# VectorE's order in the FFN loops: the low part of the next w13 weights is moved to right behind u's low part, ahead of the two adaLN accumulates and w2's low part

## What is computed

```
def swiglu(h, w13, w2):
    a, b = jnp.split(h @ w13, 2, axis=-1)
    return (jax.nn.silu(a) * b) @ w2

for layer in range(DEPTH):                       # DEPTH = 2
    mod = (cond @ ada_w[layer] + ada_b[layer]).reshape(B_, N_MOD, D)      # cond = silu(c), N_MOD = 9
    h = modulate(rmsnorm(x, norm_g[layer, 0]), sh1, sc1)
    x = x + 0.5 * g1 * swiglu(h, ff_w13[layer, 0], ff_w2[layer, 0])
    h = modulate(rmsnorm(x, norm_g[layer, 1]), sh2, sc2)
    x = x + g2 * (even_mixer(h) or multiscale_pool(h))
    h = modulate(rmsnorm(x, norm_g[layer, 2]), sh3, sc3)
    x = x + 0.5 * g3 * swiglu(h, ff_w13[layer, 1], ff_w2[layer, 1])
```

## Time and profile before

| | us |
|---|---|
| median of 3 runs | 1084.23 |
| lowest, highest | 1082.85, 1085.43 |
| span of the profiled execution | 1077.9 |
| TensorE matmul busy in it | 979.4 (91%) |
| VectorE busy | 733.9 (68%) |
| ScalarE busy | 441.3 (41%) |
| loads from HBM | 237.54 MB |

### The profile page before, as it was taken

How to read it: one execution, slowest core, us unless ns; L and a number is a source line. 1 busy time by engine, 2 the same in 40 slices (tenths; PEclk the granted TensorE clock), 3 DMA queues, 4 the chain that set the end, 5 groups by cost and what they waited for, 6 DMA issues and landing times.

```text
span 1077.9 us, 17128 instructions
## 1 busy us (share of the span) xinstructions
PE 979.4 (91%) x6656; PEld 893.6 (83%) x6656; DVE 733.9 (68%) x843; ACT 441.3 (41%) x578; POOL 123.6 (11%) x182
## 2 busy tenths in 40 slices
PE   1598999998979898999999989989999879999998
PEld 1487899997969458998998969879989769999997
DVE  4966778678887544875867867668677675555544
ACT  1424343335536343543444444234333544443432
POOL 1110111102541101110101011101110010000000
PEclk9999999998989699899999989999999989999999
DMA  9986888886734022787887747868787416456441
GB/s 339 343 309 229 277 297 297 290 217 223 242 104 131 1 98 98 269 287 284 282 302 262 270 158 257 308 232 307 277 291 275 149 42 235 164 188 202 148 156 39
DMA packets 155690, 239.19 MB, mean 222 GB/s; under 512 B 14464, under 2 KB 124928, under 8 KB 155520
## 3 DMA queue, kind: packets, MB, share of 16 engines
q1 hardware_dynamic: 135056, 166.81, 46.0%
q0 software_dynamic: 19440, 71.31, 18.2%
q10 hardware_dynamic: 1152, 0.49, 0.2%
HBM read 237.54 MB, written 1.05 MB: 221 GB/s over the span
## 4 chain that ended last, share of the span: by engine, by line
PE 42%; DMA 25%; DVE 18%; issue 6%; ACT 5%; SPq 3%; POOL 1%; ACTq 0%; DVEq 0%; POOLq 0%
PE ps L1106 25%; DMA raw<-in_ff_w 24%; DVE lo L703 6%; DVE acc L744 4%; PE ps L1148 3%; PE ps L1147 3%; PE ps L1151 3%; SPq L296 2%; PE ps L1258 2%; DVE lo L709 1%; DVE x L793 1%; ACT arena L487 1%; PE ps L1261 1%; DVE xn L789 1%; ACT hi L455 1%
## 5 line engine op out<-in xcount | busy, mean ns | idle before, releaser
L1106 PE MATMUL ps<-hT_hi,hi 128*128 128x256 f32 x1408 | 402.0, 286 | 11.1 <-DVE lo L703 6.6
L1106 PE MATMUL ps<-hT_lo,hi 128*128 128x256 f32 x1408 | 400.5, 284 | 0.0
L1106 PE MATMUL ps<-hT_hi,lo 128*128 128x256 f32 x1408 | 400.3, 284 | 0.0
L1106 PEld LDWEIGHTS ps<-hT_hi,hi 128*128 128x128 f32 x1408 | 272.2, 193 | 19.4 <-DVE lo L703 10.5
L1106 PEld LDWEIGHTS ps<-hT_lo,hi 128*128 128x128 f32 x1408 | 272.4, 193 | 2.7
L1106 PEld LDWEIGHTS ps<-hT_hi,lo 128*128 128x128 f32 x1408 | 272.2, 193 | 0.0
L703 DVE TENSOR_TENSOR lo<-raw,hi 128x2048 fp32r<-128x2048 f32 (+1 forms) x110 | 243.8, 2216 | 16.2 <-ACT hi L455 15.5
L455 ACT ACTIVATE hi<-raw 128x2048 fp32r<-128x2048 f32 (+1 forms) x106 | 200.2, 1889 | 31.2 <-DMA raw<-in_ff_w 17.5
L511 ACT ACTIVATE hi<-raw 128x1024 fp32r<-128x1024 f32 x88 | 93.4, 1061 | 276.6 <-DMA raw<-in_ff_w 142.7
L720 DVE TENSOR_TENSOR u_lo<-u_buf,u_hi 128x256 fp32r<-128x256 f32 x88 | 37.3, 424 | 212.6 <-ACT u_hi L504 212.5
L744 DVE SCALAR_TENSOR_TENSOR acc<-ada,cond,acc 128x1024 f32<-128x1024 f32 x115 | 147.0, 1279 | 0.7
(11 more groups left out here) (126 smaller groups left out, 891.2 us busy)
## 6 DMA issues: line engine op xcount, KB each, us to landing
raw<-in_ff_w SPq DMA_DIRECT2D x86, 1024.0 KB, 7.6
ada<-in_ada_w POOLq DMA_DIRECT2D x132, 512.0 KB, 6.7
raw<-in_ff_w SPq DMA_DIRECT2D x92, 512.0 KB, 8.5
raw<-in_w_in SPq DMA_DIRECT2D x12, 1024.0 KB, 8.0
arena<-in_ada_w SPq DMA_DIRECT2D x4, 1024.0 KB, 18.8
raw<-in_w_out SPq DMA_DIRECT2D x4, 1024.0 KB, 6.3
raw<-in_ada_w SPq DMA_DIRECT2D x2, 1024.0 KB, 15.0
arena<-in_b_rpb SPq DMA_DIRECT2D x16, 128.0 KB, 4.2
```

Of the source, the lines that this page charges most:

```text
L1106: ins = mm(out, a, b, start=first and m == 0, stop=last and m == len(pairs) - 1)
```

## The change

In the loop body of VectorE's FFN, four instructions of each step change places. Before: `u_mul`, accumulate, `u_low`, accumulate, `w2_low`, `split_lo`. Now: `u_mul`, `u_low`, `split_lo`, accumulate, accumulate, `w2_low`. In FFN 3, without accumulates, only `w2_low` and `split_lo` change places. Nothing is added or removed, and the programs of the other engines and queues stay as they are, as do all waits.

```
                         u_mul(Q - 1, 4 * i, first=isinstance(i, int) and i + d == 0)
+                        u_low(Q - 1, 4 * i)
+                        split_lo(n0 + d + 2, 4 * i)
                         if with_ada:
                             ada_tile(m0, 2 * d, i, gates)
-                        u_low(Q - 1, 4 * i)
-                        if with_ada:
                             ada_tile(m0, 2 * d + 1, i, gates)
                         w2_low(Q, 4 * i)
-                        split_lo(n0 + d + 2, 4 * i)
                     if with_ada:
                         mod_out(m0, i)
```

## The result

The changed kernel takes 1131.09 us (median of 4 runs, 1124.57 to 1132.01), the kernel before, beside it, 1083.54 us (4 runs, 1075.36 to 1085.43). The ratio is 1.0464, with a 95% interval of 1.0406 to 1.0522 (the two medians alone give 1.0439). The forecast of 1104.6 us had the sign and the place, but the time lies 10 us above its range. The profiled execution has a span of 1129.6 us, 51.7 us more than before. Ratios are formed from the faster executions of each kernel alone; the traces of the second and the fifth experiment come from slower ones (1078.02 and 1145.74 us).

The account below looks back on a forecast made before the run. TensorE (91% busy) was taken to bound the kernel, losing 1.6 us a turn to the load round. Adding 14.8 us for twelve turns and 5.6 for first turns to 1084.2 gave 1104.6 us, range 1094 to 1121.

Parts of the forecast that it names:

- The round of VectorE and ScalarE: From one u_high to the next, when only these two engines are waited for: 8.60 us, about TensorE's 8.5.
- The round through mod_sum: From one mod_sum to the next, TensorE waits for the last accumulate: 37.79 us a turn against 36.55, plus 14.8 us.
- The clock: Rival: TensorE's waits at mod_sum let its clock fall to 1.2 GHz, 27 us more, 1132 us; chance 0.04.
- w2's load: First w2 load of a half turn, behind the pair: lands 11.2 us after split_lo, needed at 11.7; no cost.
- the w2 load is late too: Rival: the forecast plus a late w2 load, 1.1 us more in 15 turns, 1121 us; chance 0.11.
- First turns: First turn of each of FFNs 0 to 2: mod_sum starts later, plus 5.6 us in all.
- FFN 3: The FFN without accumulates: w2_low fits into VectorE's gaps while w2_high waits for TensorE; no cost.
- the forecast itself: The main case, the longer round through mod_sum and longer first turns: 1096 to 1117 us, chance 0.74.
- No change: Rival: VectorE has room to spare, so its order does not show; about 1084 us, chance 0.05.
- faster: Rival: the load round decides, the earlier split_lo gains 0.87 us twice a turn, 19 us, some 1065 us; chance 0.06.

Follow-up runs that it names:

- the second: Changed kernel with the last step of each turn put back in the order of before (u_mul, accumulate, u_low, accumulate, w2_low, split_lo): 1064.2 us, ratio 0.9821.
- the fifth experiment: Changed kernel with w2_low moved ahead of split_lo, both accumulates still behind split_lo: 1133.8 us, ratio 1.0479 to the kernel before.
- last experiment: Changed kernel with adaLN loads in the loops cut to 128 of 1024 columns (thin loads), no filling work: 1111.4 us, ratio 1.0312.
- third experiment: Changed kernel with TensorE's mod_sum moved behind the w2 of the last step: 1076.73 us, ratio 0.9958 to the kernel before.
- fourth experiment: Changed kernel with 26 more identity transposes on TensorE ahead of each mod_sum: 1108.94 us, ratio 1.0304 to the kernel before.
- eighth experiment: Kernel before with each half turn's first w2 load issued ahead of the pair of w13 loads on SyncE's queue: 1045.92 us, ratio 0.9729.
- first experiment: Kernel before with only w2_low and split_lo changing places in VectorE's step: 1097.62 us, ratio 1.0122.

## Why the prediction was wrong

**The round of VectorE and ScalarE: right.** 8.60 us were forecast, 8.57 measured. The two accumulates take 1.31 us from start to start (799.47 to 800.78), near the 1.39 taken and within its bounds.

**The round through mod_sum: right.** It is 37.65 us, against 37.79 (last experiment). The path was the one named: mod_sum waits for the last accumulate in all 15 turns (2.57 to 5.06 us), and moving either side of that wait, the accumulates or mod_sum, takes the loss away (second and third experiment). Over 36.55 us this term is 13.2 us; forecast 14.8. The 36.55 hold 1.7 us of late loads that the longer turn swallows; over the 34.88 of a turn without them the round costs 2.8 us a turn.

**The clock: the step that failed.** The prediction had it as a rival with a chance of 0.04, "a turn or two of it" within the range, because FFN 1's four turns showed 1.00 with as much waiting. But those four turns hold five waits, 4.85 us together, the longest 1.67 us at mod_sum, and the change put a wait of 2.6 to 5.1 us in one place in every turn. The row that should have counted was the one turn of before with a clock of 0.95: it begins behind a wait of 1.86 us at mod_sum, shorter than the 2.9 forecast for every turn. It would have told that a fall is likely, and not how often, since the 2.49 us at 85.47 had none behind them. The clock fell at 13 of 15 mod_sums, 25.4 us; the range had room for two falls, 3 us. The fourth experiment confirms this by another way: with the waits filled, the time is 17 to 22 us lower. The Trainium skill, "TensorE: Matmul & The Clock Gate", section "What's actually happening", says that the clock is throttled unless activity lifts it; I had cited it and given it 4 in 100. The trace agrees with it as far as that goes: transposes of up to 1.97 us behind the waits, 1.04 to 1.09 us at 14 of the 15 mod_sums with work in front of them.

**w2's load: set at nothing, and it was not.** I had reckoned a landing 11.2 us after split_lo, and a need at 11.7. In the nine turns in which w2_high waits for this load (the last of each FFN has no such wait) it lands 12.2 to 12.4 us after split_lo in six, and 12.8, 13.4 and 14.0 us after it in three. Each of these nine turns is longer than 37.65 us and the fall at its start by just the landing less 11.5 to 11.6 us, from 0.7 us to 2.5, 10.1 us together. So the need was forecast well and the landing too early, by 1 us in most turns. The sum counted two adaLN loads (1.05 MB) ahead of w2's. The DMA views from split_lo's end to the landing, in a usual turn (591.33 to 603.73 us) and in the one shown above (779.93 to 793.96), q1 being SyncE's queue and q0 GpSimd's with adaLN (packets, MB, share of the DMA engines' time):

```profile
q1 hardware_dynamic: 2242, 2.66, 62.9%
q0 software_dynamic: 320, 1.15, 27.8%
...
q1 hardware_dynamic: 2224, 2.62, 54.6%
q0 software_dynamic: 510, 1.84, 36.5%
```

In the usual turn the bytes are about those of the sum, and the load is 1 us later all the same. In the late one a third adaLN load has come in: GpSimd's timeline shows three issued at 776.73, 781.78 and 783.08, and two more at 790.34 and 791.65, before w2's load landed at 793.98. They are in a queue of their own and don't stand behind it. The DMA view of 787 to 790 us shows both queues moving at once:

```profile
q0 software_dynamic: 219, 0.77, 66.1%
q1 hardware_dynamic: 380, 0.41, 39.1%
```

What remains of the twelve turns, 484.89 less 12 x 37.65 less the 22.7 of the clock, is 10.4 us, and that is this term: 10.1 in the nine turns, and 0.2 in the three without such a wait. The rival "the w2 load is late too" had priced it at 1.1 us a turn, with a chance of 0.11; it is 0.87 us.

**First turns: right.** From an FFN's first w13 on TensorE to its first mod_sum they took 42.46, 39.05 and 41.03 us before and take 44.01, 42.37 and 42.77 now, 6.6 us more; 5.6 were taken. The first w2 load does land sooner, which puts the second step's u_high 2.1, 1.2 and 2.5 us sooner after that w13; but from there to mod_sum are 26.08, 25.29 and 25.29 us instead of the 24.43 reckoned, since w2's next load is late here too.

**FFN 3: nearly right.** From its first w13 to the end are 195.86 us, 1.2 more than before; nothing was forecast. Its first 10 us have a granted clock of 0.78 (1.00 before); from 929 to 1112 us it is 0.98, and TensorE is busy 182.16 of 183.00 us.

**The sum.** The twelve turns: 13.2 (round) + 22.7 (clock) + 10.4 (loads) = 46.3. With 6.6 in the first turns and 1.2 in FFN 3, less 2.3 in the stretches between the FFNs, that is 51.8, against the 51.7 us between the two spans. The 2.3 are a remainder: 2.7 us of falls behind the last mod_sums of FFN 0 and 1 are in it, and the stretch from FFN 0's last mod_sum to FFN 1's first w13 is 4.9 us shorter (198.51 against 203.40), for which no run gives a cause. The forecast had the round and the first turns, 20.4 us; they measured 19.8. (The low end of the forecast itself stands in the prediction as 1096 and as 1094 us; its terms give 1094.) The rival "the clock falls" named 1132 us and the result is 1131, but that is luck, a sum of other terms: it left the loads out and had the clock in all 15 turns at 1.8 us.

**No change, and faster: wrong.** VectorE is busy 66% of the span and its order costs 4.6%. The Trainium skill, "Perfetto Trace Analysis", section "Identifying the Most-Contended Engine", which the prediction weighed, says to improve the engine with the highest occupancy first. The trace doesn't contradict it: that engine is TensorE (88%), and its waits are what costs. What was wrong was to read from it that an engine at 66% may be put in any order. And a larger reserve of the kernel before lay in the order of SyncE's queue: 2.7% by the eighth experiment, some 26 of its 35 us in the turns of FFNs 0 to 2.

## What to carry to other kernels

A wait of the busiest engine costs more than its length when its clock falls with it. Where a change gathers the busiest engine's slack into one wait, price the fall for each occurrence, not for one or two; and look whether the waiting engine has other work to put in front of the wait.

When engines hand work round, write down the longest round through each place where the busiest engine waits, one distance at a time. Here that gave 37.79 against 37.65 us, while a look at busy shares alone would have said that nothing happens.

A small load that is needed first should not stand behind a large one that is needed later. And another queue's loads don't wait their turn: count those issued until the small load lands, not only those issued ahead of it.

## What the runs showed of the hardware

- The length of a wait alone did not tell whether the clock falls, nor for how long. In the changed kernel 3.29 us (529.94) was followed by a stretch 2.5 us longer, 5.06 us (802.20) by one only 1.3 us longer, and 3.23 us (762.04) by none. With thin loads, waits of the same 2.55 us were followed by 0, 1.4 or 1.6 us. What decides was not settled.
- In some of these the clock is still full when the wait ends and falls later: there the eight transposes take 1.09 us, and only matmuls behind them are longer, as at 820.75 us of the last experiment (transposes 1.09, a w2 matmul 0.63 instead of 0.39).
- 26 transposes of 128x128 with nothing to wait for take 3.00 us. Put in front of mod_sum, they left one fall in 15 places instead of 13, and made the kernel 17 to 22 us faster.
- How the two queues share the DMA engines depends on the moment. From 787 to 790 us GpSimd's moved 0.77 MB and SyncE's 0.41; from 533.5 to 536.5 us it was 0.90 MB against 0.28 ("q0 software_dynamic: 235, 0.90, 77.1%").
- Among the loads of 0.5 MB that the text follows, each issued right behind a pair of 2 MB, the landing came 8.4 us after the issue at the least (changed kernel, 745.42) and 13.6 us at the most (first experiment, 560.55).
